# Two layers of a transformer trunk with product-key experts: expert rows beside the keys, and the modulation at the experts' begin

## What is computed

```python
def peer_ffn(h, wq, subkeys, u, v):          # per block of 128 tokens
    q = (xc @ wq).reshape(C, PEER_HEADS, 2, PEER_DKEY // 2)
    s = jnp.einsum('chzd,zkd->chzk', q, subkeys)          # 8 heads, 2 halves, 128 keys
    top_s, top_i = lax.top_k(s, PEER_TOPK)                # 16 of each half
    cand_s = top_s[:, :, 0, :, None] + top_s[:, :, 1, None, :]
    best_s, best_j = lax.top_k(cand_s, PEER_TOPK)         # 16 pairs = 16 experts a head
    idx = take_along_axis(cand_i, best_j)
    g = jax.nn.softmax(best_s, axis=-1)
    act = gelu(einsum('cd,chkd->chk', xc, take(u, idx)))
    return einsum('chk,chkd->cd', g * act, take(v, idx))
```

## Time and profile before

| | us |
|---|---|
| median of 3 runs (4769.70 to 4795.25) | 4771.01 |
| the profiled execution, by its own time | 4783.03 |
| its span, first to last instruction | 4781.4 |
| TensorE busy | 4179.8 |
| VectorE busy | 3339.1 |
| ScalarE busy | 1307.1 |
| GpSimd busy | 1767.5 |

### The profile page before, as it was taken

How to read it: one execution, slowest core, us unless ns; L and a number is a source line. 1 busy time by engine, 2 the same in 40 slices (tenths; PEclk the granted TensorE clock), 3 DMA queues, 4 the chain that set the end, 5 groups by cost and what they waited for, 6 DMA issues and landing times.

```text
span 4781.4 us, 53394 instructions
## 1 busy us (share of the span) xinstructions
PE 4179.8 (87%) x18407; PEld 2873.7 (60%) x18407; DVE 3339.1 (70%) x6731; ACT 1307.1 (27%) x2628; POOL 1767.5 (37%) x1652
## 2 busy tenths in 40 slices
PE   7999976694999899999999979886657779999997
PEld 3676664483676666666666645553443446666665
DVE  2466665568889677777777846775588767777776
ACT  3231311111666211111111123331214652222222
POOL 0012111022665455566565600000126655454452
PEclk8999978797999999999999989998778989999998
DMA  6966774713999999999999926888518999999995
GB/s 235 286 198 200 228 224 140 262 58 106 360 408 346 389 363 400 396 389 390 368 390 391 392 99 189 227 222 233 181 52 320 381 365 398 391 389 400 394 393 224
DMA packets 514579, 1408.04 MB, mean 294 GB/s; under 512 B 45693, under 2 KB 128893, under 8 KB 509471
## 3 DMA queue, kind: packets, MB, share of 16 engines
q1 hardware_dynamic: 330014, 733.73, 46.0%
q0 software_dynamic: 184320, 671.17, 36.2%
HBM read 1226.46 MB, written 178.26 MB: 294 GB/s over the span
## 4 chain that ended last, share of the span: by engine, by line
PE 65%; DVE 14%; DMA 10%; ACT 3%; POOL 3%; issue 3%; SPq 0%; DVEq 0%; ACTq 0%; POOLq 0%
PE ps L1840 20%; PE ps L1831 17%; DMA peer_arena<-in_peer_u 4%; PE ps L1804 3%; PE ps L1518 3%; DMA u_rows<-mixer_arena 3%; PE ps L746 3%; PE ps L1227 2%; PE ps L1232 2%; DMA expert_rows<-u_rows,peer_arena 2%; PE ps L321 2%; PE ps L749 2%; DVE expert_rows L2085 2%; PE ps L815 1%; DMA u_rows<-hidden 1%
## 5 line engine op out<-in xcount | busy, mean ns | idle before, releaser
L1787 POOL DMA_INDIRECT expert_rows<-u_rows,peer_arena x640 | 829.1, 1296 | 1052.5 <-DVE expert_rows L2085 821.8
L1831 PE MATMUL ps<-part_arena,peer_part_arena 128*128 128x384 f32 (+1 forms) x4096 | 1031.4, 334 | 37.7 <-DVE peer_part_arena L2128 25.4
L2085 DVE SCALAR_TENSOR_TENSOR expert_rows<-expert_rows,mixer_in 128x1024 f32<-128x1024 f32 x640 | 762.2, 1220 | 114.3 <-DMA expert_rows<-u_rows,peer_arena 112.0
L1794 POOL DMA_INDIRECT expert_rows<-in_peer_v,peer_arena x640 | 742.5, 1160 | 223.9 <-issue 186.5
L1831 PEld LDWEIGHTS ps<-part_arena,peer_part_arena 128*128 128x128 f32 x4096 | 699.7, 190 | 110.1 <-issue 99.0
L1840 PE MATMUL ps<-best,peer_arena 128*128 128x512 f32 x1540 | 685.3, 592 | 0.0
L1831 PE MATMUL ps<-mixer_in_parts,peer_part_arena 128*128 128x384 f32 (+1 forms) x2048 | 633.7, 309 | 0.0
L2110 DVE SCALAR_TENSOR_TENSOR peer_arena<-expert_rows,peer_arena 128x1024 f32<-128x1024 f32 x445 | 571.7, 1285 | 35.0 <-DVE peer_arena L2110 1.9
L1804 PE MATMUL ps<-expert_rows,peer_arena 128*128 128x512 f32 x768 | 387.8, 653 | 202.9 <-ACT peer_arena L1919 202.7
L1840 PEld LDWEIGHTS ps<-best,peer_arena 128*128 128x128 f32 x1540 | 285.1, 189 | 296.0 <-issue 296.0
L1571 POOL TENSOR_TENSOR part_arena<-peer_arena,part_arena 128x1024 fp32r<-128x1024 f32 x32 | 76.5, 2392 | 1007.1 <-ACT part_arena L1548 1007.1
(11 more groups left out here) (273 smaller groups left out, 6104.7 us busy)
## 6 DMA issues: line engine op xcount, KB each, us to landing
peer_arena<-in_peer_u SPq DMA_DIRECT2D x256, 512.0 KB, 12.1
best<-in_peer_v SPq DMA_DIRECT2D x154, 512.0 KB, 8.2
mixer_arena<-in_peer_u SPq DMA_DIRECT2D x272, 256.0 KB, 7.4
u_rows<-mixer_arena SPq DMA_DIRECT2D x136, 512.0 KB, 5.0
hidden<-in_peer_u SPq DMA_DIRECT2D x240, 256.0 KB, 6.2
u_rows<-hidden SPq DMA_DIRECT2D x120, 512.0 KB, 5.1
gates<-peer_arena SPq DMA_DIRECT2D x20, 2048.0 KB, 10.7
peer_arena<-in_peer_v SPq DMA_DIRECT2D x52, 512.0 KB, 7.6
```

The costliest lines, as they stand in the source:

```text
L1787: pool.indirect_dma_start(u_ring[:, k % U_SLOTS, :], None, u_table, bass.IndirectOffsetOnAxis(u_index[s][:, m:m + 1], 0)).then_inc(u_row_i ...
L1794: pool.indirect_dma_start(v_ring[:, k % V_SLOTS, :], None, v_table, bass.IndirectOffsetOnAxis(v_index[s][:, m:m + 1], 0)).then_inc(v_row_i ...
L1831: mm = pe.matmul(ps[:, 6, 0:dense_tok], left[j % len(left)][:, c, :], right[:, c, :], start=at == 0, stop=at == len(todo) - 1)
L2085: dve.scalar_tensor_tensor(out=rows, in0=rows, scalar=1.0, in1=B.x[:, :, rows_at + s * P:rows_at + s * P + P], op0=ALU.mult, op1=ALU.mult, ...
```

## The change

`Early` holds, for each layer, what is done in the keys stage: heads chosen, groups of products, of gelus, of shares and of sums, and rows of `u` and of `v` gathered.

- **Keys.** A new stage `keys_and_rows` takes the place of `product_keys` in both layers. Its steps are written out instead of looped. Behind step 3 VectorE chooses for heads 0 and 1 of the first sparse tile (32 experts). Behind steps 5 to 15 it multiplies one group of `u` rows each, 22 rows in all. Eight groups get their gelus and shares there. In layer 1 TensorE also sums six groups (behind steps 10 to 15); in layer 0 none. POOL gathers 26 rows of `u` in either layer and 16 rows of `v` in layer 1, into slots of their own (four for `u`, four for `v`). The PSUM banks of queries and scores are laid out anew, so that banks 2 and 3 are free for the sums. The iota is loaded here and stays.
- **Experts.** `choose(0)` is for the six other heads, in one part instead of two, and eight groups (11 to 18) go at pieces 0, 3, 5, 8, 10, 13, 15, 18 of `choose(0)` and `choose(1)` together. Groups 19 to 47 go beside the lots.
- **Modulation.** Of the 48 tiles of `w_mod` for layer 1, 24 are now loaded and multiplied at the start of layer 0's experts, two tiles a load in two slots (`front`), 16 beside its lots, one in front of every fourth, and 8, the last gate, at the start of layer 1's experts. On TensorE they stand ahead of all sums of the stage.

```diff
+Early = collections.namedtuple("Early", "heads groups gelus shares sums u_rows v_rows")
+EARLY = (Early(2, 11, 8, 8, 0, 26, 0), Early(2, 11, 8, 8, 6, 26, 16))
+CHOSEN_BEHIND, EARLY_FROM = 3, 5
+U_EARLY, V_EARLY = 4, 4
...
-            keys = make(product_keys, layer, segs)
+            keys = make(keys_and_rows if EARLY[layer].heads else product_keys, layer, segs)
...
+def keys_and_rows(B, layer, segs):
...
+    def group_at(j):
+
+        return j - EARLY_FROM
...
+        pe.wait_ge(const_in, 16 * layer + 16)
+        project(0)
+        for j in range(STEPS):
+            if j + 1 < STEPS:
+                project(j + 1)
+            score(j)
+            if 0 <= group_at(j) - 5 < E.sums:
+                spread(group_at(j) - 5)
...
+        split_w(0)
+        split_w(1)
+        for j in range(STEPS):
+            take(j)
+            if j + 2 < STEPS:
+                split_w(j + 2)
+            if j == CHOSEN_BEHIND + 1:
+                exp()
+            if group_at(j) >= 3:
+                gelus(group_at(j) - 3)
+            if 0 <= group_at(j) - 5 < E.sums:
+                diagonals(group_at(j) - 5)
+
...
+        for j in range(STEPS):
+            split_low(j)
+            if group_at(j) >= 1:
+                gather_u(group_at(j) - 1)
+            if E.v_rows and group_at(j) >= 6:
+                gather_v(group_at(j) - 6)
+        for a in range(group_at(STEPS) - 1, E.u_rows // GROUP):
+            gather_u(a)
+            if a - 5 < E.v_rows // GROUP:
+                gather_v(a - 5)
...
+        def products(a):
+            for k in range(GROUP * a, GROUP * a + GROUP):
+                dve.wait_ge(u_row_in[k % U_SLOTS], 16 * ((before + k) // U_SLOTS) + 16)
+                rows = S.u_row(k).rearrange("p (c d) -> p c d", c=C)
+                dve.scalar_tensor_tensor(out=rows, in0=rows, scalar=1.0, in1=B.x[:, :, rows_at:rows_at + P],
+                                         op0=ALU.mult, op1=ALU.mult, accum_out=S.score[0][:, k:k + 1]).then_inc(score_ok, 1)
...
+        for j in range(STEPS):
+            strongest(j)
+            if j == CHOSEN_BEHIND:
+                choose()
+            if group_at(j) >= 0:
+                products(group_at(j))
+            if 0 <= group_at(j) - 2 < E.shares:
+                shares(group_at(j) - 2)
...
+    AHEAD_AT = (0, 3, 5, 8, 10, 13, 15, 18) if E.heads else (16, 18, 20, 22, 24, 25)
+    AHEAD, EXP_FIRST = len(AHEAD_AT), 3 if E.heads else 0
+    G0, K0, SUMMED = E.groups, GROUP * E.groups, GROUP * E.sums
+    late, PARTS = slice(E.heads, HEADS), 1 if E.heads else 2
     top, top_key = best_of(B, tiles)
...
+    FRONT, MOD, FRONT_EACH = (3 * C, C)[layer], (2 * C, 0)[layer], 2
+    mod = ModTiles(B, (ar, Arena(y_tok[1])), "mod", 9 * C, 1, ps[:, 5, 2 * FRONT:2 * FRONT + 2 * MOD]) if MOD else None
+    front_space = Arena(B.peer_arena)
+    front_space.at = at
+    front = ModTiles(B, (front_space, front_space), "front", (6 * C, 11 * C)[layer], FRONT_EACH, ps[:, 5, 0:2 * FRONT])
...
-        return range(AHEAD + (FIRST - AHEAD) * lot // BATCH, AHEAD + (FIRST - AHEAD) * (lot + 1) // BATCH)
+        at = G0 + AHEAD
+        return range(at + (FIRST - at) * lot // BATCH, at + (FIRST - at) * (lot + 1) // BATCH)
...
+        for n in range(FRONT // FRONT_EACH):
+            front.load(sp, n, n % 2)
         if mod:
+            if E.v_rows:
+                sp.wait_ge(s0_mm, E.v_rows - SUMMED)
             for n in range(2):
                 mod.load(sp, n, n)
         for n in range(nd * P // TG):
             if mod:
-                for m in range(4 * n + 2, min(4 * n + 6, MOD)):
...
     def gpsimd(pool):
-        for k in range(steps):
+        for k in range(E.v_rows, steps):
             s, m = divmod(k, PAIRS)
-            if m == 0:
-                pool.wait_ge(index_ok, s + 2 if s else 1)
-            elif k == PAIRS // 2:
+            if k == E.heads * TOPK:
+                pool.wait_ge(index_ok, 1)
+            elif k == PAIRS // 2 and PARTS == 2:
                 pool.wait_ge(index_ok, 2)
-            if k >= U_SLOTS:
-                pool.wait_ge(score_ok, k - U_SLOTS + 1)
-            pool.indirect_dma_start(u_ring[:, k % U_SLOTS, :], None, u_table,
-                                    bass.IndirectOffsetOnAxis(u_index[s][:, m:m + 1], 0)).then_inc(u_row_in[k % U_SLOTS], 16)
-            if k >= V_SLOTS:
+            elif m == 0 and k:
+                pool.wait_ge(index_ok, s + PARTS)
+            if k >= E.u_rows:
+                if k - U_SLOTS >= K0:
+                    pool.wait_ge(score_ok, k - U_SLOTS + 1 - K0)
+                pool.indirect_dma_start(S.u_row(k), None, u_table,
+                                        bass.IndirectOffsetOnAxis(u_index[s][:, m:m + 1], 0)).then_inc(u_row_in[k % U_SLOTS], 16)
+            if k - V_SLOTS >= SUMMED:
...
             pe.sem_inc(mod.used, 2)
             pe.wait_ge(mod.added, 1)
-        for a in range(AHEAD - 1):
+        pe.sem_inc(front.used, 2)
+        for n in range(FRONT // FRONT_EACH):
+            front.multiply(pe, n, n % 2, n * FRONT_EACH)
+        for a in range(E.sums, G0 + AHEAD - 1):
             spread(a)
         turn(0)
         for n in range(nd):
             for x in range(LOTS):
                 at = n * LOTS + x
-                if mod and at % 2 == 0 and at // 2 < MOD:
-                    mod.multiply(pe, at // 2, at // 2 % 2, at // 2)
+                if at % 4 == 0 and at // 4 < MOD:
+                    mod.multiply(pe, at // 4, at // 4 % 2, at // 4)
                 lot(at)
                 if x == TURN_AT and n + 1 < nd:
...
+        for a in range(E.gelus, G0):
             gelus(a)
-            if a:
-                diagonals(a - 1)
+        for a in range(E.sums, G0 - 1):
+            diagonals(a)
+        for n in range(AHEAD):
+            if n == EXP_FIRST:
+                exp(0)
+            gelus(G0 + n)
+            if G0 + n:
+                diagonals(G0 + n - 1)
+        exp(1)
...
+        for piece, _ in enumerate(itertools.chain(choose(0), choose(1))):
+            if piece in AHEAD_AT:
+                products(G0 + ahead)
+                for a in range(G0 + ahead - 1 if ahead else E.shares, G0 + ahead):
+                    shares(a)
                 ahead += 1
         assert ahead == AHEAD
+        if E.v_rows:
+            dve.wait_ge(s0_mm, E.v_rows - SUMMED)
         turn(0)
         for n in range(nd):
```

More of the change, by code:

```diff
@@ L453, in norm @@
     if split:
-        ar.take(KEYS_AHEAD)
+        ar.at = PEER_KEPT + KEYS_AHEAD
     t0, n = segs[0][0], sum(s[1] for s in segs)
@@ new lines, in search_pairs @@
+def search_pairs(dve, chain, settle, here, best, best_j, cand):
+    heads = range(here.shape[1])
+    for to, a, b in pairs_that_may_win(here[:, :, 0, :], here[:, :, 1, :], cand[0]):
+        chain.inc(dve.tensor_tensor(to, a, b, ALU.add))
+    chain.wait(dve)
+    yield
+    settle(dve)
+    for h in heads:
+        chain.inc(dve.max(best[:, h, 0:8], cand[0][:, h, :]))
+    chain.wait(dve)
+    yield
+    settle(dve)
+    for h in heads:
+        chain.inc(dve.max_index(best_j[:, h, 0:8], best[:, h, 0:8], cand[0][:, h, :]))
+        chain.inc(dve.match_replace(cand[1][:, h, :], best[:, h, 0:8], cand[0][:, h, :], LOWEST))
+        if h % 4 == 3 or h == heads[-1]:
+            chain.wait(dve)
+            yield
+            settle(dve)
+    for h in heads:
+        chain.inc(dve.max(best[:, h, 8:16], cand[1][:, h, :]))
+    chain.wait(dve)
+    yield
+    settle(dve)
+    for h in heads:
+        chain.inc(dve.max_index(best_j[:, h, 8:16], best[:, h, 8:16], cand[1][:, h, :]))
+    chain.wait(dve)
+    yield
+    settle(dve)
@@ L1753, in sync @@
             if mod:
-                for m in range(4 * n + 2, min(4 * n + 6, MOD)):
+                for m in range(2 * n + 2, min(2 * n + 4, MOD)):
                     mod.load(sp, m, m % 2)
@@ L2136, in vector @@
             dve.sem_inc(mod.added, 1)
-        dve.wait_ge(iota_in, 16)
-        for _ in choose(0):
-            pass
+        if not E.heads:
+            dve.wait_ge(iota_in, 16)
         ahead = 0
-        for piece, _ in enumerate(choose(1)):
-            if piece in (0, 2, 4, 6, 8, 9):
-                products(ahead)
-                if ahead:
-                    shares(ahead - 1)
+        for piece, _ in enumerate(itertools.chain(choose(0), choose(1))):
[3 more added lines that the diff above has]
+                    shares(a)
                 ahead += 1
         assert ahead == AHEAD
+        if E.v_rows:
+            dve.wait_ge(s0_mm, E.v_rows - SUMMED)
         turn(0)
```

432 lines of the change are left out of this document (306 added, 126 removed).

## The result

| | before | after |
|---|---|---|
| median, us | 4773.83 | 4887.53 (4870.66 to 4895.85, 4 runs) |
| ratio, 95% interval | | 1.0224 [1.0204, 1.0243] |
| span of the profiled execution | 4781.4 | 4883.2 |
| TensorE busy | 4179.8 | 4260.7 |
| mean granted TensorE clock | 0.925 | 0.916 |

What follows compares the result with a forecast made beforehand. TensorE was taken to bound the first layer's keys and most of its lots, DMA the second's lots. Layer terms 30 + 86 - 74 and 42 + 29 - 74 gave +39 on 4771: 4810 us, whole range 4755 to 4878.

Steps and rivals of the forecast that it cites:

- Keys, +30 and +42: Written-out keys stages of the first and second layer: early choices and products make them 30 and 42 us longer.
- Front, layer 0, +86: First layer's experts, start to first lot: modulation ahead of the sums makes it 158 us against 72, +86.
- f: Time at which TensorE has done its modulation at a front: 62 us in the first layer, 28 in the second.
- Rival 1: Clock stays low at the front: f = 86 and 33, +24 and +5, 4839 us; chance 0.15.
- The rule of the Trainium skill: Front modulation: short matmul bursts between DMA waits are throttled again and again, so it would run at 1.2 GHz throughout.
- VectorE's stall: First layer's front: VectorE idle for 80 to 90 us, with POOL's u row as its releaser.
- Lots, layer 0, -74: First layer's lots: VectorE becomes the longest engine at 268 us, and the lots take 292 instead of 366, -74.
- The upper end of 332: First layer's lots: their longest forecast time, 332 us, if VectorE keeps the 64 us of gaps it has.
- Front, layer 1, +29: Second layer's experts, start to first lot: 8 modulation tiles and the rest take 102 us against 73, +29.
- Lots, layer 1, -74: Second layer's lots: DMA and VectorE have less to do, 210 us, between 188 and 250, -74.
- Dense passes, 0: Dense passes and the rest: no change, since their rows and tiles are the same.
- the upper end of 4878: Whole kernel: top of the whole range, 4878 us, from upper ends of both fronts, second keys and one lots stretch.

Runs made afterwards that it cites:

- experiment 8: The changed kernel with all modulation back beside layer 0's lots, and GpSimd issuing u rows ahead of waiting v rows: 4791.03 us, ratio to before 1.0021.
- experiment 11: The changed kernel with the scaling of a lot's first token left out in both layers: 4885.11 us, ratio to before 1.0227.
- experiment 10: The changed kernel with the 16 modulation tiles beside layer 0's lots neither loaded nor multiplied: 4867.59 us, ratio to before 1.0194.
- experiment 6: The changed kernel with two unread 512-column matmuls ahead of each load of two modulation tiles at the fronts: 4901.23 us, ratio to before 1.0260.
- experiments 3 and 9: 3: early rows in layer 1 alone, modulation beside layer 0's lots, 4754.13 us; 9: the same, last u and v rows issued in the experts, 4752.48 us.

## Why the prediction was wrong

The direction and the mechanism held; three of six terms held in size, and the largest was too small.

- **Keys, +30 and +42:** +27 and +40. VectorE sets layer 0's steps and TensorE the second layer's last ones, as forecast: 9.80 us a step (3630.89, 3640.68 and 3650.48 in the chain are the starts of projections). Of the end (6.55 and 10.04 us in GpSimd's queue) I had the issues alone, 3 and 5 us, and not that the meeting waits until the rows have landed. And the 6.87 us of a step before are 103.0 us over 15 steps, where these two rows are 14 steps and most of the last one; a step took 6.98.
- **Front, layer 0, +86: +121. This is the step that failed**, and in it the value f = 62 us for TensorE's modulation. I took 6.6 us a pair for the first two and 4.3 for the rest, from 3.36 at the high clock, because at 6.6 TensorE would never wait for a load, and because stretches without breaks stood at 0.95 to 1.00. TensorE did wait for no load, from 1192.9 on, and the clock stayed at 0.50. f was 90. Of the 28 us, 25 are the last ten pairs at 6.84 us instead of 4.3; the rest is the start, where the third load took 9.44 us instead of 4.7 and TensorE waited 2.7 for it. All behind f came close to what was worked out: first lot at f + 99, forecast f + 96. Rival 1, f = 86, was this case; it had a chance of 0.15 and a time of 4839, and its lots kept my value.
- **Why the rows misled.** The stretches at 0.95 to 1.00 were full of wide matmuls. The multiplication at 1.68 us stood beside lots and sums. The one row where TensorE worked on little but tiles of the modulation, 651 to 686 us, said 0.50, and I explained it by its waits. The rule of the Trainium skill that I cited (TensorE: Matmul & The Clock Gate, "HAM oscillation — how this bites in real kernels") would make the front slow as well, but by waits between bursts; the 68.43 us row has no waits and the clock is low all the same. The result came out as by the rule, and not for its reason.
- **VectorE's stall:** forecast 80 to 90 us with a `u` row as releaser. It was 104.1 us with a gelu as releaser. In experiment 8, without the modulation in front, an earlier `u` row made the front 6 us shorter and left the wait for the gelu.
- **Lots, layer 0, -74: -53.** I had VectorE's busy time as bound, 268 of 292. It is busy 269 of 313. ScalarE has no effect to speak of (experiment 11), and TensorE, 252 busy at 0.91 against a forecast 242, or its loads still hold part of the time (experiment 10). Whether VectorE holds the rest wasn't tried. The upper end of 332 held it.
- **Front, layer 1, +29: +38**, 6 of them f (33.6 instead of 28), again the low clock, 0.50 for all of its 28 us. **Lots, layer 1, -74: -73.** **Dense passes, 0:** 996.95 of 1000 us busy from 1700 to 2700.

In sum 61 us of error: 35 in layer 0's front, 21 in its lots, 9 and 1 in layer 1's, and 5 the other way in the keys. 39 + 61 = 100 us on 4771 are 4871, still under the upper end of 4878. The measured median is 16 us higher. Nearly all of that is the 12 us by which I went down from the profiled execution to a median, and which doesn't hold for the changed kernel: its profiled execution (4885.08) is 102 us above the one before (4783.03) and 2.5 below its own median. The rivals were laid out as if one thing could go wrong at a time: rival 1 with these lots is 4839 + 21 = 4860, and no rival had both. The upper end doesn't come out of its own parts either. Both upper fronts, the upper second keys and one upper lots stretch are 24 + 5 + 10 + 40 = 79 us, 4889 and not 4878.

## What to carry to other kernels

Work that nobody waits for may stand ahead on an in-order queue only until the moment at which the first awaited instruction becomes ready, so measure that moment (38 us here: 8 tiles free, 14 cost 13 us, 24 cost 45), and measure it again after any change that makes the awaited work ready sooner: here an earlier start of the rows turned a wait-filler of 31 us that cost nothing into one that cost all of it. Time fillers at the clock that their own kind of matmul ran at when it was alone, not at the one it had in mixed company. And do the same edit per layer: early rows gained 23 us in the layer whose lots left TensorE and VectorE idle and lost 42 in the one where TensorE was full.

## What the hardware did that I had not expected

- TensorE worked on 128x2 matmuls for 68.43 us with no gap and was granted 1.2 GHz throughout. The same instructions, 0.214 us apiece there, took 0.105 among lots and sums and 0.116 between wide matmuls (3.71/32, experiment 6). In a regular mixture of both, never idle, the granted clock still changed from one level to the other, and stayed at the lower from 1222 to 1280 us (experiment 6).
- At the end of a stage the drain on GpSimd's queue ended 1.6 to 1.8 us after the last gathered row had landed, and 6.1 to 6.3 us after that row's issue (experiments 3 and 9). With the last four issues moved behind the meeting, the experts began 8.6 us sooner after the last search of the keys.
